# Windowed attention in a two-layer encoder trunk: the scores of its first two query blocks stand between the last projections

## The chip, the cores and the metric

The kernel runs on one core of a Trainium2 chip. The metric is the device time of one execution in microseconds (us). The profile names the engines: PE is TensorE (matmuls; PEld its weight loads), DVE is VectorE, ACT is ScalarE, POOL is GpSimd and SP issues the transfers.

## The reference

The program is a trunk of two layers on 1024 tokens of width 1024: windowed grouped-query attention, a mixture of experts, differential attention, a second mixture, and a final norm. The change touches the windowed attention alone, the first stage of the program:

```python
h = rmsnorm(x, norm_mix[0])
qkv = h @ w_qkv                       # 16 heads of queries, 4 of keys, 4 of values, 64 wide
# for each block i of 128 queries: its own 128 keys and the 128 on either side
logits = einsum('bqkgd,bskd->bkgqs', qi / 8, kb) - slopes * dist
logits = where(valid & (dist <= 128), logits, -inf)
m = max(max(logits), sink)
p = exp(logits - m)
probs = p / (sum(p) + exp(sink - m))
out[i] = einsum('bkgqs,bskd->bqkgd', probs, vb)
x = x + out @ w_o
```

## The kernel before

**The stage.** `windowed_attention` first normalises and turns the eight tiles of `x`. Then it works through four groups, one for each key/value head with the four query heads that share it. The first and the last group are written out, and the second and third are the two turns of a loop. In each group come six projections and then eight blocks of 128 queries. After the groups the output projection (`OutProjection`) adds the result to `x`.

**Six projections.** `Projections.tensor` makes projection `o` with 24 matmuls of 512 columns (eight slices of the width by three products, lines 363 to 365: every fp32 operand is kept as a high and a low part). `projections.order` gives what each makes: query heads 0 and 1, query heads 2 and 3, keys and values, first for the first 512 tokens (o = 0, 1, 2), then for the last 512 (o = 3, 4, 5). The text counts them as first to sixth. The first five eighths of the first projection stand at the group's start, and the rest (`AHEAD`) between the last blocks of the group before. ScalarE takes each result out of its PSUM bank as the high part (`q_parts` line 608, `k_hi` line 612) and VectorE takes the low part (lines 723 and 726); of the third and the sixth, ScalarE also copies keys and values together into `kvT` (line 613), a corner of the buffer `pT`. Semaphores count these steps: `proj_done`, `hi_ready`, `parts_ready`.

**PSUM.** The eight banks are `S` (four), `TB` (two) and `O` (two). Before the change the first four projections go to the banks of `S`, the fifth and sixth to `O`:

```python
projected = lambda o: S[:, o, :] if o < 4 else O[:, o - 4, :]
```

The scores of a block need all four banks of `S`, one for each query head.

**A block.** `head_scores(i)` on TensorE makes two matmuls for each head (line 790): 256 keys wide for blocks 0 and 7, 384 for the others. VectorE adds the bias and takes the maximum (`masked_scores`, line 690; its last step, `a_snk`, frees the exponentials), ScalarE takes four exponentials and that of the sink (`exponentials`, lines 596 and 598), and VectorE divides (`normalise`, line 705). `product(i)` on TensorE turns the probabilities one key tile at a time into the two banks of `TB` (line 803), ScalarE copies each turned tile into `pT` (line 630), and TensorE multiplies them with the values (line 810) into `O`; VectorE takes the block out (`heads_out`, line 712). The values are turned by `value_rows(0)` (first 512 tokens) and `value_rows(1)` (last 512): TensorE line 775 out of `kvT`, VectorE line 678.

**Order.** Each engine's order is written out by hand in its `group` function. TensorE runs the scores two blocks ahead: `head_scores(i + 2)` stands before `product(i)`. The scores of one block wait, head by head, until VectorE has read the block before (`biased`). ScalarE and VectorE also cut the next group's weights into high and low parts (`high_part`, line 405, `low_part`, line 411), a third of the slice at a time. In the last group ScalarE cuts one slice of the output weights for each block instead (line 472), with the low part on GpSimd (line 476).

## Time and profile before

| | us |
|---|---|
| median of 3 runs | 2544.45 |
| lowest, highest | 2537.21, 2546.45 |
| the profiled execution | 2540.93 |
| its span, first to last instruction | 2538.9 |
| PE busy | 2313.7 (91%) |
| DVE busy | 1866.3 (74%) |
| ACT busy | 1549.1 (61%) |
| POOL busy | 299.8 (12%) |
| mean granted TensorE clock | 0.957 of full speed |

A row of the timeline gives the start of an instruction in us from the span's start, its length, the engine, the line, what it writes and reads, how often it is repeated, and in brackets the idle time before it and what ended that. The end of a matmul is modelled and overlaps the next one's start, so the pace of TensorE is read from start to start. Buffers are named without the stage's prefix `a0_`: `a_S` are the score banks, `a_TO` are `TB` and `O` together, and the probabilities are `shared`. The four groups begin at about 31, 117, 202 and 287 us, and the output projection at 374 us.

### The profile page before, as it was taken

To read this page: it belongs to the slowest core of one execution; us is meant where nothing else is said; L and a number is where in the kernel's file an instruction comes from. 1 tells how busy PE (TensorE), PEld (TensorE's weight loads), DVE (VectorE), ACT (ScalarE), POOL (GpSimd) and SP (SyncE) were. 2 spreads that over 40 slices of the span, in tenths; PEclk is the share of its full clock that TensorE was granted. 3 is DMA by queue.
4 is the path that set the end of the run, shared out by engine and by line. 5 is a ranking of instruction groups with operands and counts; after the bars stand their busy time and mean duration, and the time that the engine had idled before them with its cause. 6 is when DMAs were issued, how large, how long until landed. Compare 5 with 4: busy or idle time off the path is not lost. (4 is left out here: it accounts for less than half of the span.)

```text
span 2538.9 us, 34343 instructions
## 1 busy us (share of the span) xinstructions
PE 2313.7 (91%) x11448; PEld 1754.4 (69%) x11448; DVE 1866.3 (74%) x2483; ACT 1549.1 (61%) x2037; POOL 299.8 (12%) x260
## 2 busy tenths in 40 slices
PE   7999989779999999948999999998967999999992
PEld 5667758657777777637888888886855777777771
DVE  5765582678898988857666676656277988989885
ACT  5554461448787777735566665555045787877872
POOL 0000020012121211130000000002001221212102
PEclk9999999979999999979999999999988999999996
DMA  3004021479999999962000000002148999999995
GB/s 125 26 22 135 25 67 53 166 248 402 393 400 397 394 401 392 401 209 93 26 25 25 25 25 17 8 25 75 45 166 288 398 401 396 402 396 396 402 388 211
DMA packets 132051, 538.62 MB, mean 212 GB/s; under 512 B 25776, under 2 KB 54576, under 8 KB 82832
## 3 DMA queue, kind: packets, MB, share of 16 engines
q1 hardware_dynamic: 113040, 470.67, 48.6%
q0 software_dynamic: 18944, 67.12, 7.6%
q8 instruction: 35, 0.57, 0.1%
q14 instruction: 32, 0.26, 0.0%
HBM read 487.54 MB, written 50.20 MB: 212 GB/s over the span
## 5 line engine op out<-in xcount | busy, mean ns | idle before, releaser
L1694 DVE TENSOR_TENSOR m_lo_gate<-m_raw_gate,m_hi_gate 128x2048 fp32r<-128x2048 f32 x132 | 297.6, 2290 | 79.9 <-ACT m_hi_gate L1689 79.0
L1694 DVE TENSOR_TENSOR m_lo_up<-shared,m_hi_up 128x2048 fp32r<-128x2048 f32 x128 | 292.4, 2286 | 3.6 <-ACT m_hi_up L1689 3.4
L1694 DVE TENSOR_TENSOR m_lo_down<-m_raw_down,m_hi_down 128x2048 fp32r<-128x2048 f32 x124 | 279.0, 2282 | 6.1 <-ACT m_hi_down L1689 6.1
L1689 ACT CAST m_hi_down<-m_raw_down 128x2048 fp32r<-128x2048 f32 x124 | 236.2, 1906 | 34.4 <-DMA m_raw_down<-in_moe_w_down_dram 30.5
L1689 ACT CAST m_hi_gate<-m_raw_gate 128x2048 fp32r<-128x2048 f32 x132 | 246.4, 1908 | 10.7 <-DMA m_raw_gate<-in_moe_w_gate_dram 10.6
L1689 ACT CAST m_hi_up<-shared 128x2048 fp32r<-128x2048 f32 x128 | 244.5, 1912 | 12.9 <-DMA shared<-in_moe_w_up_dram 12.1
L1811 PE MATMUL m_G<-m_hi_gate,m_x_hi 128*96 128x512 f32 x512 | 205.6, 402 | 11.3 <-DVE m_x_lo L1921 11.3
L1698 POOL DMA_INDIRECT m_xg<-hn_rows,m_pick x62 | 158.9, 2562 | 415.8 <-PE m_XT L1824 415.8
L1811 PE MATMUL m_U<-m_hi_up,m_x_hi 128*96 128x512 f32 x512 | 205.2, 401 | 0.0
L1812 PE MATMUL m_G<-m_hi_gate,m_x_lo 128*96 128x512 f32 x512 | 205.2, 401 | 0.0
L1813 PE MATMUL m_G<-m_lo_gate,m_x_hi 128*96 128x512 f32 x512 | 203.7, 398 | 0.0
L1812 PE MATMUL m_U<-m_hi_up,m_x_lo 128*96 128x512 f32 x512 | 201.9, 394 | 0.0
L1813 PE MATMUL m_U<-m_lo_up,m_x_hi 128*96 128x512 f32 x512 | 200.3, 391 | 0.0
L1811 PE MATMUL m_Y<-m_hi_down,m_h_hi 128*96 128x512 f32 x496 | 198.6, 400 | 0.0
L1812 PE MATMUL m_Y<-m_hi_down,m_h_lo 128*96 128x512 f32 x496 | 195.1, 393 | 0.0
L1813 PE MATMUL m_Y<-m_lo_down,m_h_hi 128*96 128x512 f32 x496 | 194.6, 392 | 0.0
L1407 DVE CUSTOM_DVE_ANT_0 shared<-a_S,a_bias 128x1024 f32<-128x1024 f32 x128 | 151.6, 1222 | 22.2 <-PE a_S L1525 11.9
L1308 ACT ACTIVATE shared<-shared 128x1024 f32<-128x1024 f32 x128 | 146.1, 1144 | 29.1 <-DVE shared L1412 27.3
L363 PE MATMUL a_S<-a1n_hi,a_w_hi 128*128 128x512 f32 x384 | 155.9, 406 | 0.0
L364 PE MATMUL a_S<-a1n_hi,a_w_lo 128*128 128x512 f32 x384 | 152.6, 397 | 0.0
L365 PE MATMUL a_S<-a1n_lo,a_w_hi 128*128 128x512 f32 x384 | 152.6, 397 | 0.0
L1892 ACT ACTIVATE m_gated<-m_G,zero_col 96x512 f32<-96x512 f32 x64 | 43.8, 684 | 157.2 <-PE m_G L1813 156.8
(385 smaller groups left out, 4989.8 us busy)
## 6 DMA issues: line engine op xcount, KB each, us to landing
m_raw_gate<-in_moe_w_gate_dram SPq DMA_DIRECT2D x128, 1024.0 KB, 9.8
shared<-in_moe_w_up_dram SPq DMA_DIRECT2D x128, 1024.0 KB, 11.9
m_raw_down<-in_moe_w_down_dram SPq DMA_DIRECT2D x124, 1024.0 KB, 10.9
out_rows<-m_y POOLq DMA_DIRECT2D x64, 384.0 KB, 8.0
a1n_rows<-in_diff_w_qkv_dram SPq DMA_DIRECT2D x21, 512.0 KB, 5.3
out_rows<-gain_b SPq DMA_DIRECT2D x1, 8064.0 KB, 37.2
x_res<-in_x_dram SPq DMA_DIRECT2D x4, 1024.0 KB, 10.0
a0n_rows<-in_swa_w_o_dram SPq DMA_DIRECT2D x8, 512.0 KB, 3.6
```

Source lines behind the costliest of these rows:

```text
L363: pe.matmul(out, left[0], right[0], start=first, stop=False)
L364: pe.matmul(out, left[1], right[0], start=False, stop=False)
L365: return pe.matmul(out, left[0], right[1], start=False, stop=last)
L1308: last = act.activation(row, row, ACT.Exp, bias=neg2[:, i % 2, c:c + 1], accum_out=sum2[:, i % 2, c:c + 1])
L1407: dve.tensor_tensor_reduce(probs[:, i % 2, c, :].rearrange("p (a b) -> p a b", a=2), S[:, 2 * c:2 * c + 2, :], bias[:, at:at + T].rearrang ...
L1689: act.copy(self.hi[w][:, cut], self.raw[w][:, cut]).then_inc(self.hi_done[w], 1)
L1694: eng.tensor_tensor(self.lo[w][:, cut], self.raw[w][:, cut], self.hi[w][:, cut].bitcast(F32), ALU.subtract)\
L1698: pool.indirect_dma_start(out=self.xg[:, :], out_offset=None, in_=self.hn_rows, in_offset=bass.IndirectOffsetOnAxis(rows, 0)).then_inc(sel ...
L1811: pe.matmul(out[n], l_hi[:, rows], r_hi[:, cols], start=(k == 0), stop=False)
L1812: pe.matmul(out[n], l_lo[:, rows], r_hi[:, cols], start=False, stop=False)
L1813: last = pe.matmul(out[n], l_hi[:, rows], r_lo[:, cols], start=False, stop=(k == K - 1))
L1892: act.activation(gated[:, :], G[0:CAP, :], ACT.Silu, bias=t.zero_col[0:CAP, :]).then_inc(gated_done, 1)
```

## The change

- Projections 4 to 6 go to other banks: the fourth to `O[0]`, the fifth to `TB[1]`, the sixth to `O[1]`. `S[3]` takes no projection any more.
- TensorE makes the scores of block 0 and the first half's value rows behind the fourth projection instead of the fifth, and the scores of block 1 behind the fifth instead of the sixth. The scores of block 2 follow the sixth at once. The second half's value rows stand behind the product of block 0, no longer before the scores of block 2.
- ScalarE takes the exponentials of block 0 behind the fourth projection's queries and those of block 1 behind the fifth's. It copies block 0's turned tiles before it takes the sixth projection out.
- VectorE does the same for its steps, and normalises block 1 before the sixth projection's low part. The low parts of the next group's weights move: the first third behind block 0's scores, the second into block 2; the last third stays in block 4.
- `kvT` lies in the other half of `pT`, and TensorE's waits for parts and value rows are set to the new order.

```diff
--- before.py
+++ after.py
@@ -524,7 +524,7 @@
         v_rows = sb("a0_v_rows", [P, NT, 2, HEAD], F32)
         probs = t.shared[:, :].rearrange("p (a b n) -> p a b n", a=3, b=QH)
         pT = sb("a0_pT", [P, 2, 3, QH * P], F32)
-        kvT = pT[:, 0, 0:2, :].rearrange("p a b -> p (a b)")
+        kvT = pT[:, 1, 0:2, :].rearrange("p a b -> p (a b)")
         bias = sb("a0_bias", [P, QH, WIN], F32)
         dist = sb("a0_dist", [P, WIN], F32)
         far = sb("a0_far", [P, WIN], F32)
@@ -546,7 +546,7 @@
 
         sink_loaded = t.sem("a0_sink_loaded")
 
-        projected = lambda o: S[:, o, :] if o < 4 else O[:, o - 4, :]
+        projected = lambda o: (S[:, 0, :], S[:, 1, :], S[:, 2, :], O[:, 0, :], TB[:, 1, :], O[:, 1, :])[o]
         proj_done, hi_ready, parts_ready = projections.done, t.sem("a0_hi_ready"), t.sem("a0_parts_ready")
         v_turned, v_rows_ready = t.sem("a0_v_turned"), t.sem("a0_v_rows_ready")
         scores, scores_seen, biased = t.sem("a0_scores"), t.sem("a0_scores_seen"), t.sem("a0_biased")
@@ -599,7 +599,15 @@
                            .then_inc(exp_done, 1)
 
 
+                    def turned_out(i):
+                        for j in range(tiles[i]):
+                            c = TILES * g + before[i] + j
+                            act.wait_ge(p_turned, c + 1)
+                            act.copy(pT[:, i % 2, j, :], TB[:, (before[i] + j) % 2, :]).then_inc(pT_ready, 1)
+
                     for o in range(6):
+                        if o == 5:
+                            turned_out(0)
                         act.wait_ge(proj_done, 6 * g + o + 1)
                         (j, n), out = projections.order[o], projected(o)
                         cols = slice(n * HALF, (n + 1) * HALF)
@@ -613,21 +621,19 @@
                             act.copy(kvT[:, cols], out).then_inc(hi_ready, 1)
                         if n == 1 and j < 2 and not last_group:
                             projections.high_part(act, g + 1, j)
-                        if o == 4:
-                            exponentials(0)
+                        if o in (3, 4):
+                            exponentials(o - 3)
 
                     for i in range(NT):
-                        if i + 1 < NT:
+                        if 2 <= i + 1 < NT:
                             exponentials(i + 1)
                         if last_group:
                             out_proj.high_weights(act, i)
                         n = 8 * g + i
                         if i >= 2:
                             act.wait_ge(pv_done, n - 1)
-                        for j in range(tiles[i]):
-                            c = TILES * g + before[i] + j
-                            act.wait_ge(p_turned, c + 1)
-                            act.copy(pT[:, i % 2, j, :], TB[:, (before[i] + j) % 2, :]).then_inc(pT_ready, 1)
+                        if i >= 1:
+                            turned_out(i)
                         if i == 3 and not last_group:
                             projections.high_part(act, g + 1, 2)
 
@@ -714,6 +720,9 @@
 
 
                     for o in range(6):
+                        if o == 5:
+                            masked_scores(2)
+                            normalise(1)
                         dve.wait_ge(hi_ready, 6 * g + o + 1)
                         (j, n), out = projections.order[o], projected(o)
                         cols = slice(n * HALF, (n + 1) * HALF)
@@ -726,23 +735,23 @@
                                 last = dve.tensor_tensor(k_lo[part, cols], out[0:64],
                                                          k_hi[0:64, cols].bitcast(F32), ALU.subtract)
                         last.then_inc(parts_ready, 1)
-                        if n == 1 and j < 2 and not last_group:
-                            projections.low_part(dve, g + 1, j)
-                        if o == 4:
+                        if o == 3:
                             masked_scores(0)
                             value_rows(0)
+                            if not last_group:
+                                projections.low_part(dve, g + 1, 0)
                             normalise(0)
-                    for i in range(NT):
+                        if o == 4:
+                            masked_scores(1)
+                    value_rows(1)
+                    heads_out(0)
+                    for i in range(2, NT):
                         if i + 1 < NT:
                             masked_scores(i + 1)
-                        if i == 0:
-                            value_rows(1)
-                        else:
-                            normalise(i)
-                        if i >= 1:
-                            heads_out(i - 1)
-                        if i == 4 and not last_group:
-                            projections.low_part(dve, g + 1, 2)
+                        normalise(i)
+                        heads_out(i - 1)
+                        if i in (2, 4) and not last_group:
+                            projections.low_part(dve, g + 1, i // 2)
                     if last_group:
                         o_part(0)
                         o_part(1)
@@ -780,7 +789,7 @@
                         n = 8 * g + i
                         a, b = blocks[i]
                         if i == 0:
-                            pe.wait_ge(parts_ready, 6 * g + 4)
+                            pe.wait_ge(parts_ready, 6 * g + 3)
                         if i == 3:
                             pe.wait_ge(parts_ready, 6 * g + 6)
                         for h in range(QH):
@@ -831,22 +840,26 @@
 
 
 
-                        if o == 4:
+                        if o == 3:
                             pe.wait_ge(parts_ready, 6 * g + 1)
                         projections.tensor(pe, out, g, o, first_group)
-                        if o == 4:
-
-
+                        if o == 3:
                             head_scores(0)
                             value_rows(0)
-                    head_scores(1)
-                    value_rows(1)
+                        if o == 4:
+                            head_scores(1)
                     for i in range(NT):
                         if i + 2 < NT:
                             head_scores(i + 2)
                         if i == 0:
+                            pe.wait_ge(v_rows_ready, 2 * g + 1)
+                            pe.wait_ge(parts_ready, 6 * g + 5)
+                        if i == 1:
+                            pe.wait_ge(parts_ready, 6 * g + 6)
                             pe.wait_ge(v_rows_ready, 2 * g + 2)
                         product(i)
+                        if i == 0:
+                            value_rows(1)
 
                 group(0, True, False)
                 with pe.Fori(1, KV - 1) as g:
```

ScalarE in the first group, from the second third of the weights on, before:

```order
L405 CAST a_w_hi<-a0n_rows 128x8x128
L593 ISA
L596 ACTIVATE shared,a_sum<-shared,a_neg 128x256 x4
L598 ACTIVATE a_exs<-a_snk,zero_col 128x4
L603 REGISTER_ALU
L612 CAST a_k_hi<-a_TO 64x512 x2
L613 COPY a_pT<-a_TO 128x512
L593 REGISTER_ALU
L596 ACTIVATE shared,a_sum<-shared,a_neg 128x384 x4
L598 ACTIVATE a_exs<-a_snk,zero_col 128x4
L629 ISA
L630 COPY a_pT<-a_TO 128x512
```

and after the change:

```order
L405 CAST a_w_hi<-a0n_rows 128x8x128
L593 REGISTER_ALU
L596 ACTIVATE shared,a_sum<-shared,a_neg 128x384 x4
L598 ACTIVATE a_exs<-a_snk,zero_col 128x4
L605 ISA
L606 COPY a_pT<-a_TO 128x512
L605 REGISTER_ALU
L606 COPY a_pT<-a_TO 128x512
L611 REGISTER_ALU
L620 CAST a_k_hi<-a_TO 64x512 x2
L621 COPY a_pT<-a_TO 128x512
```

Block 1's exponentials (384 wide) and block 0's two turned tiles stood behind the sixth projection's keys (`a_k_hi`, and `a_pT` at line 613), and now stand ahead of them.

VectorE in the first group, around the sixth projection's low part of the keys, before:

```order
L702 RECIPROCAL a_inv<-a_sum 128x4
L62 REGISTER_ALU
L705 TENSOR_SCALAR shared<-shared,a_inv 128x256 x4
L717 REGISTER_ALU
L726 TENSOR_TENSOR a_k_lo<-a_TO,a_k_hi 64x512 x2
L74 ISA
L690 ISA shared,a_top<-a_S,a_bias 128x384
```

and after the change:

```order
L708 RECIPROCAL a_inv<-a_sum 128x4
L62 REGISTER_ALU
L711 TENSOR_SCALAR shared<-shared,a_inv 128x384 x4
L726 REGISTER_ALU
L735 TENSOR_TENSOR a_k_lo<-a_TO,a_k_hi 64x512 x2
L681 REGISTER_ALU
L684 COPY a_v_rows<-a_TO 128x4x64 x2
```

Before, block 0's division (256 wide) came ahead of the keys' low part and block 1's masked scores behind it. Now block 1's division (384 wide) comes ahead of it, and the second half's value rows behind it.

TensorE in the first group, from the end of block 2's scores on, before:

```order
L790 MATMUL a_S<-a_k_hi,a_q_parts 128x384
L790 MATMUL a_S<-a_k_lo,a_q_parts 128x384
L803 MATMUL a_TO<-ident,shared 128x128 x8
L810 MATMUL a_TO<-a_pT,a_v_rows 128x512 x2
L790 MATMUL a_S<-a_k_hi,a_q_parts 128x384
```

and after the change:

```order
L799 MATMUL a_S<-a_k_lo,a_q_parts 128x384
L812 MATMUL a_TO<-ident,shared 128x128 x8
L819 MATMUL a_TO<-a_pT,a_v_rows 128x512 x2
L784 MATMUL a_TO<-ident,a_pT 128x128 x4
L799 MATMUL a_S<-a_k_hi,a_q_parts 128x384
```

Block 3's scores followed block 0's product at once, and the value turn out of `a_pT` stood ahead of block 2's scores; now it stands between block 0's product and block 3's scores.

## Rows read from the trace of the kernel before

**Rows 1.** The page: TensorE's granted clock in 40 slices, in tenths of full speed.
```profile
PEclk9999999979999999979999999999988999999996
```

**Rows 2.** Timeline of TensorE, second group, from its fifth projection to block 4.
```profile
137.49 0.40 PE L363 MATMUL a_TO<-a0n_hi,a_w_hi 128*128 128x512 f32 x1
...
143.09 0.27 PE L790 MATMUL a_S<-a_k_hi,a_q_parts 128*128 128x256 f32 x1
...
144.38 0.48 PE L363 MATMUL a_TO<-a0n_hi,a_w_hi 128*128 128x512 f32 x1
...
150.07 0.34 PE L790 MATMUL a_S<-a_k_hi,a_q_parts 128*128 128x384 f32 x1
...
151.31 0.34 PE L790 MATMUL a_S<-a_k_lo,a_q_parts 128*128 128x384 f32 x1
153.40 0.66 PE L775 MATMUL a_TO<-ident,a_pT 128*128 128x128 f32 x4 [1.75 <-ACT a_pT L613]
155.41 0.69 PE L790 MATMUL a_S<-a_k_hi,a_q_parts 128*128 128x384 f32 x1 [1.35 <-DVE a_top L690]
...
163.43 1.28 PE L790 MATMUL a_S<-a_k_hi,a_q_parts 128*128 128x384 f32 x1
...
171.65 1.04 PE L803 MATMUL a_TO<-ident,shared 128*128 128x128 f32 x8
...
174.32 1.97 PE L810 MATMUL a_TO<-a_pT,a_v_rows 128*128 128x512 f32 x4
175.72 0.74 PE L790 MATMUL a_S<-a_k_hi,a_q_parts 128*128 128x384 f32 x1
```

**Rows 3.** Timeline of TensorE, first group: fifth projection and block 3's scores.
```profile
54.03 0.40 PE L363 MATMUL a_TO<-a0n_hi,a_w_hi 128*128 128x512 f32 x1
...
78.61 0.74 PE L790 MATMUL a_S<-a_k_hi,a_q_parts 128*128 128x384 f32 x1
```

**Rows 4.** Timeline of TensorE, last group: fifth projection, block 3's scores, block 1's product.
```profile
307.79 0.40 PE L363 MATMUL a_TO<-a0n_hi,a_w_hi 128*128 128x512 f32 x1
...
332.07 0.74 PE L790 MATMUL a_S<-a_k_hi,a_q_parts 128*128 128x384 f32 x1
...
335.17 1.12 PE L810 MATMUL a_TO<-a_pT,a_v_rows 128*128 128x512 f32 x2 [0.24 <-ACT a_pT L630]
```

**Rows 5.** Busy time in four stretches; PEclk is the column behind POOL's.
```profile
69.00:79.00 10.00, 6.80 (x25) 4.74 (x25) 9.30 (x35) 5.91 (x18) 0.00 (x0) 0.83 0.00 0
150.00:166.00 16.00, 12.36 (x43) 8.96 (x43) 11.48 (x43) 9.53 (x30) 0.00 (x0) 0.68 0.00 1
...
321.00:331.00 10.00, 6.32 (x27) 4.86 (x26) 9.40 (x35) 5.90 (x16) 0.80 (x1) 0.83 0.01 2
338.00:373.00 35.00, 28.81 (x135) 18.10 (x134) 31.68 (x91) 27.63 (x70) 14.23 (x6) 1.00 0.29 91
```

**Rows 6.** Timeline of ScalarE, second group; the last row is from the last group.
```profile
151.58 1.17 ACT L612 CAST a_k_hi<-a_TO 64x512 fp32r<-64x512 f32 x2
...
157.42 0.62 ACT L596 ACTIVATE shared<-shared,a_neg 128x384 f32<-128x384 f32 x1 [4.07 <-DVE a_snk L696]
...
159.83 0.28 ACT L598 ACTIVATE a_exs<-a_snk,zero_col 128x4 f32<-128x4 f32 x1
...
172.28 1.07 ACT L630 COPY a_pT<-a_TO 128x512 f32<-128x512 f32 x2 [0.45 <-PE a_TO L803]
...
333.56 1.04 ACT L472 CAST a0n_hi<-a0n_rows 128x1024 fp32r<-128x1024 f32 x1
```

**Rows 7.** Timeline of VectorE, second group.
```profile
153.38 1.38 DVE L726 TENSOR_TENSOR a_k_lo<-a_TO,a_k_hi 64x512 fp32r<-64x512 f32 x2 [0.24 <-ACT a_pT L613]
154.79 0.56 DVE L690 CUSTOM_DVE_ANT_0 shared<-a_S,a_bias 128x384 f32<-128x384 f32 x1
...
160.50 0.15 DVE L701 TENSOR_TENSOR a_sum<-a_sum,a_exs 128x4 f32<-128x4 f32 x1
...
160.90 1.41 DVE L705 TENSOR_SCALAR shared<-shared,a_inv 128x384 f32<-128x384 f32 x4
```

## The prediction

> **What bounds the kernel now.** I begin with the granted clock on the page [rows 1]: TensorE is at full speed nearly everywhere, with dips in the third, ninth, sixteenth and later slices. The first dips lie inside the windowed attention, the only stage that the change touches. The timeline of TensorE in the second group shows where [rows 2]. Up to block 1's scores it works without a pause. Then it waits 1.75 us for ScalarE, which has to copy the last keys and values before they can be turned, and 1.35 us for VectorE, which can read block 1's scores only behind the keys' low part. The first score matmul behind that wait lasts 0.69 us where it lasted 0.34. The table by stretches says why: between 150 and 166 us the granted clock is 0.68 in the mean [rows 5]. With two levels, 2.4 and 1.2 GHz, that is 2 × 0.32 × 16 = 10.2 us at 1.2 GHz. The first and the last group have the same two waits and 2 × 0.17 × 10 = 3.4 us at 1.2 GHz [rows 5]. Everywhere else in a group TensorE is close to busy, so a group is as long as TensorE's work plus this one hole. All later stages begin behind the attention's end, so a microsecond saved here is saved at the end.
>
> The measure of the hole is the time from the start of the fifth projection's matmuls to the start of block 3's scores. Exactly the same TensorE work lies in it before and after: two projections, three sets of scores, two value turns and block 0's product, if for "after" I count from the end of the fourth projection, where block 0's scores now begin. Before, it is 163.43 − 137.49 = 25.94 us in the second group [rows 2], and the third repeats it. In the first it is 78.61 − 54.03 = 24.58 [rows 3], in the last 332.07 − 307.79 = 24.28 [rows 4].
>
> **The same stretch after the change**, worked out on the second group, with 0 at the end of the fourth projection.
> - *Scores of block 0 and the first value turn.* They cost 144.38 − 143.09 = 1.29 us behind the fifth projection [rows 2], and 1.29 behind the fourth. Their parts are the first three projections'; the third's take 1.80 + 1.38 us [rows 6, 7] of the fourth's 5.60. So the fifth projection runs from 1.29, for 143.09 − 137.49 = 5.60 us, to 6.89.
> - *Scores of block 1.* They wait for VectorE's reading of block 0, which has all of the fifth projection's 5.60 us for it; the wait is hidden. Eight matmuls: 151.31 − 150.07 = 1.24 from the first to the eighth and 0.18 for that one, 1.42. The sixth projection runs from 8.31 to 13.91.
> - *Scores of block 2*, 1.42 again, to 15.33, if VectorE has read block 1. It takes the fifth projection's low part from about 8.8, an estimate: 2.8 for the fourth's high and low part (as for the keys, without the third copy), then for block 0 the masked scores 2.1, the exponentials 2.3 and the division 1.6, each some 0.85 of the 384-wide price below. The low part is 1.4 [rows 7], then block 1 in 157.42 − 154.79 = 2.6 [rows 6, 7], so to 12.8. It is ready 1.1 us early.
> - *Product of block 0.* TensorE turns from 15.33. ScalarE has block 1's exponentials behind it by then: they start at 12.8 and take 159.83 + 0.28 − 157.42 = 2.69 [rows 6], to 15.5. The first turned tile can be copied 172.28 − 171.65 = 0.63 after the turns start [rows 2, 6], at 15.96, and both copies take 1.07 [rows 6], to 17.03. TensorE's two products take 175.72 − 174.32 = 1.40 [rows 2] and are issued by about 18.0.
> - *The new wait.* Only now does ScalarE take out the sixth projection. From its first copy of keys to VectorE's low part it takes 153.38 − 151.58 = 1.80 [rows 6, 7], so to 18.83, and the low part takes 1.38 more [rows 7], to 20.21. Block 3's scores need it and begin at about 20.28 with 0.07 for the two hand-overs. TensorE waits about 0.9 for the value turn and 1.1 for the scores; counted as the trace does it, from a product's modelled end, that is about 0.3 and 0.9. What queues behind: on TensorE block 3's scores and block 1's product; on ScalarE the sixth projection behind the turned tiles; on VectorE the second value rows and everything of block 3.
> - *VectorE in this spot.* Block 2's scores are read while they are made, from 14.3 to 16.9, and block 1 is normalised in 160.90 + 1.41 − 160.50 = 1.81 [rows 7], to 18.7. The keys' copies are there at 18.83, so this chain has 0.1 us to spare. It is the tightest spot of the new order.
>
> So the stretch is 20.28 us. **The sum:** first group 24.58 − 20.28 = 4.30. Second and third 25.94 − 20.28 = 5.66 each. Last group 24.28 − 20.28 = 4.00, less a loss behind it: ScalarE cuts a 1.04 us slice of the output weights in each block [rows 6], and the slices of blocks 0 and 1, 2.1 us, now both stand between the keys' copies and block 1's turned tiles, together with block 2's exponentials of 2.7. That puts the first copy at 17.03 + 1.8 + 4.8 = 23.6, where TensorE offers the tile at 20.28 + 1.8 (scores behind a product, the first 0.40 longer [rows 2]) + 0.6 = 22.7. Before, block 1's product waited 0.24 [rows 4]; it will wait about 0.85 more. Last group: 3.15. Together 4.30 + 2 × 5.66 + 3.15 = **18.8 us**.
>
> *Edits at no cost.* The fourth projection now goes to an `O` bank and waits for this group's first parts, which VectorE finishes during the second projection, over 5 us ahead. The weights' second third moves on VectorE into block 2 (1.2 us); GpSimd and SP's queue keep their order, and the load of the next weights waits for the last third, which stays in block 4.
>
> *Bounds.* Without any wait the stretch would be TensorE's own issue, 1.29 + 5.60 + 1.42 + 5.60 + 1.42 + 0.9 + 1.40 + 0.35 = 17.98, worth 2.3 us more in each group: 18.8 + 9.2 = 28.0 at most. From below, the clock decides. The rows show full speed kept where waits are spread: in the last 35 us of blocks TensorE was busy 28.81 us and the clock stayed at 1.00 [rows 5]. They show it lost behind 1.75 + 1.35 = 3.1 us of waiting close together [rows 2]. The new waits, about 1.2 us counted the same way, are nearer to the first, so I take full speed.
>
> A section of the Trainium skill speaks against that: "TensorE: Matmul & The Clock Gate", A second HAM failure mode: psum-queue depth-cycling, says that short idle spells between groups of matmuls, as a kernel cycles through its PSUM banks, can send the clock back and forth. By that rule the gain would be that of the first rival; the last group's blocks, with such spells and the clock at 1.00, speak against it here.
>
> **The rivals.**
> - *The clock still falls in the new hole.* Two waits within 2 us remain, ahead of dense work. The least that a fall cost in time at 1.2 GHz was 3.4 us [rows 5], which at half speed is 1.7 us where TensorE sets the pace. In all four groups: 18.8 − 6.8 = 12.0, 2544.45 − 12.0 = 2532. For it: the spell lies behind a product that itself has short waits. Against: under half of the idle time before.
> - *VectorE shows in block 2.* The tight 0.1 us goes, and the 1.2 us moved there add up in three groups: 3.7 less, 15.1, 2529. Against: VectorE was busy 11.48 of 16 us around the hole [rows 5], and TensorE has two blocks of scores as a buffer.
> - *Slower.* The clock falls in each group at block 3's scores and stays down for 10.2 us, as it did in the second and third [rows 5]. Before, much of that lay beside waits; now it would lie on dense work, 5.1 us a group, 20.4 in all, against 18.8: slower by 1.6, 2546. It decides from 4.7 us lost a group, and becomes measurable only near 8. Against: it takes a deeper hole than the old one to hold the clock down that long under dense work.
> - *Nothing arrives.* The saving is made and given back behind the attention, by a transfer or a stage with its own start: 2544. SP issues the experts' first weights only behind the attention's last step, so I see no such start.
>
> **How the numbers follow.** Against the profiled execution's 2540.93 the sum gives 2522.1; the median of the runs lies 3.5 above that execution, and gives 2525.6. I take **2524**. Chances: forecast 0.60, clock rival (in some or all groups) 0.22, VectorE 0.10, nothing 0.05, slower 0.03. The range goes from near the bound of 28 us, 2515, to the clock rival with the runs' own spread of some 5 us, 2537. A measurement can tell about 0.5%, 12.7 us, from no change. The forecast and the VectorE rival lie beyond that, the clock rival about on it: faster 0.75, same 0.22, slower 0.03.
>
> **What would show it.** In the second group of the new trace: fifth projection's first matmul about 1.3 us behind the fourth's end; no wait before block 1's and block 2's scores; a wait for `a_pT` ahead of the value turn and one for `a_k_lo` ahead of block 3's scores, under 1.2 us each; 20.3 us from the fourth projection's end to block 3's scores; a granted clock of 1.00 there; groups some 79.5 us long instead of 85; in the last group a wait near 1 us ahead of block 1's product. Wrong would be a clock below 0.9 in these stretches, a wait ahead of block 0's turns (VectorE late with the division), or block 4's scores later than 6 us behind block 3's.

## The result, and the profile after

| | before | after |
|---|---|---|
| median of 4 runs each, us | 2543.47 (2537.21 to 2546.45) | 2519.71 (2515.79 to 2521.06) |
| profiled execution, us | 2540.93 | 2520.45 |
| its span, us | 2538.9 | 2518.4 |

The ratio is 0.9906, with a 95% interval from 0.9892 to 0.992: the changed kernel is 23.8 us faster by the medians, and 20.5 by the two profiled executions.

The page's line of the granted clock, to be held against [rows 1]:

```profile
PEclk9999999799999999959999999999978999999996
```

It hardly differs, and it can't: a slice is 63 us long, a 9 stands for 90% or more, and 3.4 us at half speed leave 97%. The lower digits, the ninth and eighteenth before and the eighth and eighteenth now, and the last three in both, lie behind the attention, which ends in the sixth slice. The prediction's opening sentences, with dips in the third and sixteenth slices and the first of them inside the attention, misread it; what carried the argument are the stretches of [rows 5], to which the fence after next answers.

The timeline of TensorE in the second group of the changed kernel (start, length, engine, line, out<-in; in brackets the idle time before and who ended it). It answers to [rows 2]. The first row is the first score matmul behind the fourth projection, the zero point of the prediction's clock:

```profile
132.32 0.28 PE L799 MATMUL a_S<-a_k_hi,a_q_parts 128*128 128x256 f32 x1
...
133.63 0.47 PE L363 MATMUL a_TO<-a0n_hi,a_w_hi 128*128 128x512 f32 x1
...
139.30 0.34 PE L799 MATMUL a_S<-a_k_hi,a_q_parts 128*128 128x384 f32 x1
...
140.72 0.39 PE L363 MATMUL a_TO<-a0n_hi,a_w_hi 128*128 128x512 f32 x1
...
146.32 0.33 PE L799 MATMUL a_S<-a_k_hi,a_q_parts 128*128 128x384 f32 x1
...
147.73 1.03 PE L812 MATMUL a_TO<-ident,shared 128*128 128x128 f32 x8
149.00 1.98 PE L819 MATMUL a_TO<-a_pT,a_v_rows 128*128 128x512 f32 x4 [0.24 <-ACT a_pT L606]
151.15 0.65 PE L784 MATMUL a_TO<-ident,a_pT 128*128 128x128 f32 x4 [0.17 <-ACT a_pT L621]
152.77 0.44 PE L799 MATMUL a_S<-a_k_hi,a_q_parts 128*128 128x384 f32 x1 [0.97 <-DVE a_k_lo L735]
...
158.35 0.74 PE L799 MATMUL a_S<-a_k_hi,a_q_parts 128*128 128x384 f32 x1
```

The two waits of 1.75 and 1.35 us are gone. In their place stand 0.24, 0.17 and 0.97 us, and the first score matmul behind them lasts 0.44 us, where it lasted 0.69. The stretch that the prediction measures, from 132.32 to 152.77, takes 20.45 us; the last row says that block 4's scores follow 5.58 us later.

The granted clock by stretches answers to [rows 5] (stretch, its length, busy time of TensorE, weight loads, VectorE, ScalarE and GpSimd, granted clock, DMA share, GB/s). These four hold the hole of each group:

```profile
69.00:79.00 10.00, 8.48 (x40) 5.26 (x39) 9.56 (x37) 7.31 (x18) 0.00 (x0) 1.00 0.00 0
147.00:163.00 16.00, 14.15 (x71) 9.62 (x70) 14.95 (x50) 11.58 (x33) 0.00 (x0) 1.00 0.01 2
226.00:242.00 16.00, 14.16 (x69) 9.40 (x68) 14.94 (x51) 11.60 (x32) 0.00 (x0) 1.00 0.00 1
304.00:320.00 16.00, 13.17 (x67) 9.16 (x65) 14.92 (x49) 14.21 (x37) 4.98 (x3) 1.00 0.20 66
```

**Where the 21 us came from.** Every group has one mark, the fifth projection's start before and block 0's scores after; the time between two marks is one group. The attention ends where the output projection's first matmul starts (before, then after):

```profile
374.23 0.50 PE L363 MATMUL a_S<-a0n_hi,a_w_hi 128*128 128x512 f32 x1 [0.29 <-DVE a_w_lo L666]
```
```profile
352.80 0.50 PE L363 MATMUL a_S<-a0n_hi,a_w_hi 128*128 128x512 f32 x1 [0.29 <-DVE a_w_lo L672]
```

| | before | after | gain |
|---|---|---|---|
| first mark | 54.03 | 53.34 | 0.69 |
| first group | 83.46 | 78.98 | 4.48 |
| second group | 85.10 | 78.80 | 6.30 |
| third group | 85.20 | 78.78 | 6.42 |
| last mark to the output projection | 66.44 | 62.90 | 3.54 |
| sum | 374.23 | 352.80 | 21.43 |
| from there to the end of the span | 2164.7 | 2165.6 | -0.9 |

The gain of the first line is there ahead of everything that the change touches (in the two traces the first projection starts at 28.38 and 27.86 us), so it is taken as scatter: over all traces of this study this mark lies between 52.98 and 54.30 us. The last line is within its scatter too: over the same traces, one for each kernel, that part takes 2160.4 to 2168.3 us. A single span therefore can't show what a few us are worth, and the experiments are read at the output projection's start first, and by their medians second.

### The profile page after: what moved, and what is told of

Read it like the earlier page. It is cut to its first block and busy times, and to the rows that moved or that the text cites. A ratio compares the mean times of both kernels' runs of the same rounds, so it can differ in the third digit from the quotient of the medians.

```text
span 2518.4 us, 34348 instructions
## 1 busy us (share of the span) xinstructions
PE 2303.8 (91%) x11448; PEld 1747.6 (69%) x11448; DVE 1863.6 (74%) x2483; ACT 1551.2 (62%) x2037; POOL 309.7 (12%) x260
## 5 line engine op out<-in xcount | busy, mean ns | idle before, releaser
L1711 POOL DMA_INDIRECT m_xg<-hn_rows,m_pick x62 | 170.8, 2755 | 408.8 <-PE m_XT L1837 408.8
```

The costliest lines, as they stand in the source:

```text
L1711: pool.indirect_dma_start(out=self.xg[:, :], out_offset=None, in_=self.hn_rows, in_offset=bass.IndirectOffsetOnAxis(rows, 0)).then_inc(sel ...
```

## The experiments

Nine kernels ran. e1, e2, e6 and e7 shared one chip and its runs of the kernel before (median 2539.54), e0, e3, e4 and e5 another (2541.93), and e9 ran by itself (2541.32). Ratios are against these.

| | ratio (95%) | output projection starts | stretch in groups 1 to 4 |
|---|---|---|---|
| before | 1 | 374.23 | 24.58, 25.94, 25.95, 24.28 |
| e1, banks only | 1.0009 (0.9997 to 1.0021) | 373.15 | 24.57, 24.57, 25.94, 25.04 |
| e6, first wait filled | 0.9991 (0.9979 to 1.0003) | 372.73 | 24.58, 25.76, 24.59, 25.65 |
| e9, both waits filled | 0.9986 (0.9976 to 0.9995) | 373.01 | 24.58, 25.62, 24.58, 25.64 |
| e2, block 0 only | 0.9967 (0.9954 to 0.9979) | 365.29 | 23.26, 23.26, 23.26, 24.20 |
| e7, weights back | 0.992 (0.9897 to 0.9943) | 355.40 | 21.07, 21.17, 21.15, 20.36 |
| after, run again (e0) | 0.9913 (0.99 to 0.9927) | 353.14 | 20.34, 20.45, 20.45, 20.35 |
| e3, keys first | 0.9911 (0.9897 to 0.9925) | 355.25 | 20.33, 20.45, 20.45, 20.36 |
| e5, both first | 0.9909 (0.9894 to 0.9924) | 352.95 | 20.10, 20.10, 20.09, 20.10 |
| e4, low keys first | 0.9948 (0.9935 to 0.9962) | 361.86 | 20.22, 20.33, 20.32, 20.20 |

### What part of the change brings the gain

**e1, banks only.** The kernel before with nothing but the new banks, and the wait for the group's first parts moved to the projection that now takes `O[0]`:

```diff
-        projected = lambda o: S[:, o, :] if o < 4 else O[:, o - 4, :]
+        projected = lambda o: (S[:, 0, :], S[:, 1, :], S[:, 2, :], O[:, 0, :], TB[:, 1, :], O[:, 1, :])[o]
...
-                        if o == 4:
+                        if o == 3:
                             pe.wait_ge(parts_ready, 6 * g + 1)
```

> The kernel before with the new banks and nothing else: the fourth projection goes to O[0], the fifth to TB[1], the sixth to O[1], and TensorE's wait for this group's first parts moves from the fifth to the fourth projection; no scores, exponentials or copies are moved. My theory (the gain is the shorter chain in the hole, and the clock that stays up there; the banks only make room): the same stretch from the fifth projection's start to block 3's scores, 24.6, 25.9, 25.9 and 24.3 us in the four groups, ratio to before 1.000. Rival A (the banks themselves help or hurt, by who reads them while TensorE writes): a stretch or a projection that differs by over 0.3 us, a ratio off by over 0.002. Rival B (the clock alone brings the gain): 1.000 too, since the hole stays.

It is the kernel before, within 0.2%. The banks bring nothing of the gain; they only make room for the order. The trace has a surprise, to which I come back: in the second group the same two waits of 1.76 and 1.36 us stand in it, and yet the stretch takes 24.57 us and not 25.94, while that of the last group takes 25.04 and not 24.28. Both differ by more than the 0.3 us that the expectation named as the sign of rival A. The banks aren't needed for it: e6 and e9, with the old banks, show the like, 24.59 and 24.58 us in the third group, 25.65 and 25.64 in the last.

**e2, block 0 only.** The new banks, and block 0's scores, exponentials, reading and value turn behind the fourth projection. Block 1 stays behind the sixth:

```diff
+        projected = lambda o: (S[:, 0, :], S[:, 1, :], S[:, 2, :], O[:, 0, :], TB[:, 1, :], O[:, 1, :])[o]
...
-                        if o == 4:
+                        if o == 3:
                             exponentials(0)
...
-                        if o == 4:
+                        if o == 3:
+                            masked_scores(0)
+                            value_rows(0)
                         if n == 1 and j < 2 and not last_group:
                             projections.low_part(dve, g + 1, j)
-                            masked_scores(0)
-                            value_rows(0)
+                        if o == 3:
                             normalise(0)
...
-                        if o == 4:
+                        if o == 3:
                             head_scores(0)
                             value_rows(0)
                     head_scores(1)
+                    pe.wait_ge(parts_ready, 6 * g + 5)
                     value_rows(1)
```

> Half of the change: with the new banks, the scores, masked scores, exponentials, value rows and division of block 0 stand behind the fourth projection; block 1's scores stay behind the sixth, block 0's turned copies behind the keys. My theory: ScalarE has block 0's exponentials behind it when the sixth projection ends, so the keys come 1.4 us earlier and all behind them; the stretch from the fourth projection's end to block 3's scores is about 23.2 us (before 24.6, 25.9, 25.9, 24.3; after 20.4), the waits for a_pT and a_top are about 0.6 and 1.0 us instead of 1.75 and 1.35, and the clock stays up. Time about 2534, ratio 0.996. Rival B (the clock alone): with the clock at 1.00 the whole gain is there, 2520, ratio 0.991.

The order half of the expectation held in three groups: 23.26 us a stretch for 23.2, the first wait down to 0.44 us; the second stayed at 1.36 us, where 1.0 was expected. In the last group the stretch is 24.20 us, 0.08 less than before: there block 0's product waits for ScalarE in both kernels, 1.82 us before and 1.70 in e2. The clock half of the expectation failed. TensorE in its second group, and the first group's stretch:

```profile
149.70 0.66 PE L776 MATMUL a_TO<-ident,a_pT 128*128 128x128 f32 x4 [0.44 <-ACT a_pT L613]
151.71 0.44 PE L791 MATMUL a_S<-a_k_hi,a_q_parts 128*128 128x384 f32 x1 [1.36 <-DVE a_top L690]
...
152.19 0.51 PE L791 MATMUL a_S<-a_k_hi,a_q_parts 128*128 128x384 f32 x1
```
```profile
69.00:79.00 10.00, 8.63 (x36) 6.33 (x36) 9.22 (x37) 6.57 (x21) 0.00 (x0) 0.83 0.00 0
```

Two score matmuls run at full speed, the third lasts 0.51 us instead of 0.34: the fall comes half a microsecond behind the 1.36 us wait. 0.83 over 10 us is 3.4 us at 1.2 GHz, as in [rows 5], with under 60% of the waiting. So to halve the waiting isn't enough to keep the clock. The attention ends 8.9 us earlier than before, the whole change 21.4: moving block 1 too, with the turned copies, brings the other 12.5.

**e7, weights back.** The changed kernel with the low part of the weights' second third ahead of block 1's masked scores again, where before had it:

```diff
                         if o == 4:
+                            if not last_group:
+                                projections.low_part(dve, g + 1, 1)
                             masked_scores(1)
...
-                        if i in (2, 4) and not last_group:
-                            projections.low_part(dve, g + 1, i // 2)
+                        if i == 4 and not last_group:
+                            projections.low_part(dve, g + 1, 2)
```

> The changed kernel with one part undone: the low part of the next weights' second third stands behind the fifth projection's low part again, ahead of block 1's masked scores, instead of in block 2. My theory: 1.2 us more on VectorE ahead of block 1's scores pushes its exponentials to 149.1 instead of 147.9 in the second group, the turned copies and the keys behind them by 0.8 and block 3's scores by 0.7, in the first three groups: stretch 21.1 instead of 20.4, time 2521.8, ratio to before 0.9915. Rival (the place of that step is free, it only fills VectorE's idle time): stretch 20.4, ratio 0.9906.

Its second group (TensorE, then ScalarE):

```profile
151.05 1.98 PE L821 MATMUL a_TO<-a_pT,a_v_rows 128*128 128x512 f32 x4 [1.08 <-ACT a_pT L606]
153.20 0.66 PE L786 MATMUL a_TO<-ident,a_pT 128*128 128x128 f32 x4 [0.16 <-ACT a_pT L621]
154.71 0.44 PE L801 MATMUL a_S<-a_k_hi,a_q_parts 128*128 128x384 f32 x1 [0.85 <-DVE a_k_lo L735]
```
```profile
147.70 0.62 ACT L596 ACTIVATE shared<-shared,a_neg 128x384 f32<-128x384 f32 x1 [4.63 <-DVE a_snk L702]
...
150.42 1.07 ACT L606 COPY a_pT<-a_TO 128x512 f32<-128x512 f32 x2
```

VectorE spends 1.23 us on the weights, block 1's exponentials start that much later, and ScalarE comes to block 0's turned tiles 0.84 us late, counted from the group's mark: 21.1 us a stretch in the groups that have next weights, 20.36 in the last, which has none. The expectation held. This line of the change, which in the diff looks like tidying, is worth about 0.7 us a group, 2.3 us at the output projection with e7 against e0. Its clock stayed at 1.00, with waits of 1.08, 0.16 and 0.85 us.

### What holds the new hole

**e0**, the changed kernel once more beside e3, e4 and e5:

> The changed kernel itself, beside the three variants of it. Expected as before: ratio 0.991, stretch from the fourth projection's end to block 3's scores 20.3 to 20.5 us, clock 1.00 in the hole.

It repeated the stretches to 0.03 us, and the ratio within its interval.

**e3, keys first.** ScalarE takes the sixth projection's keys and values out before block 0's turned tiles, the old order of these two steps. The last group's first slice of output weights moves to stand with the second, so that it isn't in the hole:

```diff
                     for o in range(6):
-                        if o == 5:
-                            turned_out(0)
...
-                        if last_group:
+                        if last_group and i:
+                            if i == 1:
+                                out_proj.high_weights(act, 0)
                             out_proj.high_weights(act, i)
...
-                        if i >= 1:
-                            turned_out(i)
+                        turned_out(i)
```

> The changed kernel with one part undone: ScalarE takes out the sixth projection (keys and kvT) before it copies block 0's turned tiles, as in the kernel before. Rival (what the place of these copies decides, as the change's description has it): the copies and with them block 0's product come 1.8 us later, block 3's scores too: stretch 22.2, time up by 7. My theory after the changed kernel's trace: block 3's scores wait for VectorE, where the division of block 1 (ends 151.34 us) stands ahead of the keys' low part; TensorE has about 2 us to spare for the product. Products from 18.0 to 19.4 us behind the fourth projection's end, value turn to 19.8, scores at 20.4 as now. Stretch 20.4, same time as the changed kernel.

The stretch is the same to 0.01 us:

```profile
151.15 1.98 PE L818 MATMUL a_TO<-a_pT,a_v_rows 128*128 128x512 f32 x4 [1.49 <-ACT a_pT L606]
...
153.68 0.44 PE L798 MATMUL a_S<-a_k_hi,a_q_parts 128*128 128x384 f32 x1
```

ScalarE has the keys out at 150.60 us and VectorE, busy with block 1's division, takes them at 152.16. The wait that is printed stands ahead of the product (1.49 us), and nothing is won: VectorE's chain ends when it did. The copies' new place, a point of its own in the description of the change, is not where the gain is. The profiled execution reached the output projection 2.1 us after e0's: 0.5 us are there at the first mark, and 1.6 come in the last group (64.48 us for 62.84 from the mark on), where the clock fell at block 2's product (0.57 between 322 and 326 us). The medians differ by 1.3 us; in time the two kernels can't be told apart.

**e4, low keys first.** VectorE takes the keys' low part ahead of block 1's division:

```diff
                         if o == 5:
                             masked_scores(2)
-                            normalise(1)
...
+                    normalise(1)
                     value_rows(1)
```

> The changed kernel with VectorE's keys' low part ahead of block 1's division instead of behind it; ScalarE as in the changed kernel. My theory: the keys' copies end at 18.8 us behind the fourth projection's end, and the low part starts at 18.8 instead of 18.9, so the stretch is 20.3 and nothing else moves: same time as the changed kernel within 1 us. Rival (the division is what holds the hole open): stretch 18.9 to 19.5, 4 us less in all.

This was my worst expectation. Of the stretch itself it holds: 0.1 us shorter. But e4 is 8.65 us slower than e0 by the medians (2526.76 and 2518.11), and its attention ends 8.7 us later. The price is paid behind the stretch. TensorE, second group and last group:

```profile
156.71 1.09 PE L812 MATMUL a_TO<-ident,shared 128*128 128x128 f32 x8 [0.77 <-DVE a_v_rows L684]
...
319.93 1.94 PE L812 MATMUL a_TO<-ident,shared 128*128 128x128 f32 x8 [4.79 <-DVE a_v_rows L684]
```

Block 1's turns need the division and the value rows behind it. In the first three groups that is about 1 us each. In the last it is 4.79 us, and behind it the turns last 1.94 us instead of 1.09: the clock went too. The reason is seen on VectorE and GpSimd in the last group:

```profile
313.43 2.00 DVE L707 TENSOR_TENSOR a_sum<-a_sum,a_exs 128x4 f32<-128x4 f32 x1
...
315.68 3.49 DVE L711 TENSOR_SCALAR shared<-shared,a_inv 128x384 f32<-128x384 f32 x4
```
```profile
313.02 2.39 POOL L476 TENSOR_TENSOR a0n_lo<-a0n_rows,a0n_hi 128x1024 fp32r<-128x1024 f32 x1 [279.13 <-ACT a0n_hi L472]
316.54 2.41 POOL L476 TENSOR_TENSOR a0n_lo<-a0n_rows,a0n_hi 128x1024 fp32r<-128x1024 f32 x1 [1.13 <-ACT a0n_hi L472]
```

An addition of 128x4 numbers takes 2.00 us where it takes 0.16 elsewhere, and ends with GpSimd's subtraction, at 315.4. The division's four instructions take 3.49 us where they take 1.41 [rows 7], and they end 0.2 us behind GpSimd's second subtraction. Together that is 1.8 and 2.1 us more. In the changed kernel the last group's division of block 1 runs from 307.51 to 308.92 us, and GpSimd begins at 309.71. Its later blocks pay too, as those of the kernel before do: in both, five small additions of the last group take 0.8 to 2.1 us. What is new in e4 is that block 1's division, which its turns wait for, is held too.

So block 1's division ahead of the keys is a needed part of the change, in the last group above all: from its mark to the output projection e4 takes 68.61 us for e0's 62.84, in each of the first three groups 0.9 to 1.0 us more than e0.

**e5, both first**: both orders turned, e3's edit and e4's together.

> Both orders turned round at once: ScalarE takes out the sixth projection before block 0's turned tiles, VectorE makes the keys' low part before block 1's division. In the last group the first slice of the output weights is cut behind block 2's exponentials. My theory: the two chains only give way together. Low part ready at 18.8 us behind the fourth projection's end, block 0's product from 18.0 to 19.4, value turn to 19.8, block 3's scores at 19.8 instead of 20.4: 0.6 less in the first three groups, nothing in the last, where block 1's product waits longer for the slices; 2 us in all, about 2518 where the changed kernel has 2520. Rival (block 0's copies must stand first): 22.2 as in the other run, 7 us more.

The stretch falls to 20.10 us, not to 19.8:

```profile
150.43 1.98 PE L818 MATMUL a_TO<-a_pT,a_v_rows 128*128 128x512 f32 x4 [1.49 <-ACT a_pT L606]
152.25 0.60 PE L783 MATMUL a_TO<-ident,a_pT 128*128 128x128 f32 x4
152.60 0.42 PE L798 MATMUL a_S<-a_k_hi,a_q_parts 128*128 128x384 f32 x1
```

No wait is printed ahead of the scores: behind ScalarE's copies, TensorE's own issue now ends last. I had taken 1.40 us for the product, from [rows 2], where scores follow it. From 150.43 to 152.25 it is 1.82 with the value turn behind it: the 0.4 us that the first score matmul otherwise carries (0.74 us long instead of 0.34) are paid by whatever follows. So e3 (keys taken out earlier) wins 0.0 us in the stretch, e4 (their low part made earlier) 0.1 and e5 (both) 0.3: ScalarE's keys and VectorE's division end within 0.2 us of each other, and a third path is only some 0.3 us shorter. It is the longest in e5: ScalarE's exponentials, keys and turned tiles, for which the product still waits 1.49 us, and then TensorE's own issue. No run relieves ScalarE of that work, so what the hole would be without this path isn't shown; the prediction's bound of 17.98 us is 2.1 us away.

The expectation had 2 us less in all. The first three groups, from mark to mark, give 0.25 to 0.38 us each, and the last takes 0.8 back (63.61 us for 62.84), with waits of 0.53 and 1.42 us ahead of block 2's turns and product. In time e5 can't be told from the changed kernel; no run here is measurably faster than that.

### What the clock did

**e6, first wait filled.** The kernel before with seven matmuls into `TB[1]`, which nobody reads, behind block 1's scores. They fill the 1.75 us wait and add nothing to the path:

```diff
                     head_scores(1)
+                    for _ in range(7):
+                        pe.matmul(TB[:, 1, :], k_hi[:, 0:P], q_parts[:, 0, 0:HALF], start=True, stop=True)
                     value_rows(1)
```

> The kernel before, with seven more matmuls of 512 columns on TensorE behind block 1's scores in each group, written to the free bank TB[1] and never read: about 1.5 us of the 1.75 us wait is filled with work, no other engine's order is changed. My theory: the granted clock stays at 1.00 in the hole, but the chain over ScalarE and VectorE is as long as before. In the first and last group nothing is gained, since block 0's product waits for ScalarE's copies either way; in the second and third the product's two multiplications and block 3's first scores run at full speed, 1.9 us a group. Time about 2539.7, ratio 0.9985. Rival B (the clock alone): most of the 24 us, ratio 0.991. Rival C (the clock does not matter at all): 1.000.

**e9, both waits filled.** The same, and five more of them into `TB[0]` behind the value turn, once its bank is read:

```diff
                     value_rows(1)
+                    pe.wait_ge(v_rows_ready, 2 * g + 1)
+                    for _ in range(5):
+                        pe.matmul(TB[:, 0, :], k_hi[:, 0:P], q_parts[:, 0, 0:HALF], start=True, stop=True)
```

> The kernel before with both waits of the hole filled: seven more matmuls of 512 columns behind block 1's scores (into TB[1]) and five behind the second value turn (into TB[0], once its value rows are read), none of them read. The first fill alone left the clock to fall in two of the four groups, and where it stayed up the stretch was 24.6 us as in the first group of the kernel before. My theory (the clock's share is what the second and third group of the kernel before have over 24.6, and the time at 1.2 GHz in block 3): clock 1.00 in the hole of every group, stretch 24.6 in the first three, the output projection starts at about 370.5 us instead of 374.2, ratio 0.9985. So 17 of the 21 us that the change saves up to there are the shorter chain. Rival (the clock is worth more than that): output projection's start at 366 or less.

The ratios came out as expected (0.9991 and 0.9986 for 0.9985, though e6's interval includes 1), the mechanism only in part: e9 was to reach the output projection at 370.5 us and reached it at 373.01. The stretches of e9 in the second and the third group:

```profile
150.00:166.00 16.00, 13.59 (x60) 9.30 (x58) 12.14 (x45) 9.37 (x30) 0.00 (x0) 0.89 0.00 0
236.00:252.00 16.00, 13.33 (x63) 8.62 (x61) 14.53 (x56) 9.88 (x28) 0.00 (x0) 1.00 0.00 0
```

The clock stayed up in the first and the third group and fell in the second and the last, in e6 just so. Up to block 0's product the second and the third group of e9 read alike, with waits of 0.15, 0.18 (0.20 in the third), 0.67 and 1.41 us. Then the product, in the one and in the other:

```profile
160.32 3.44 PE L810 MATMUL a_TO<-a_pT,a_v_rows 128*128 128x512 f32 x4 [1.41 <-ACT a_pT L630]
162.78 1.31 PE L790 MATMUL a_S<-a_k_hi,a_q_parts 128*128 128x384 f32 x1
...
245.21 1.98 PE L810 MATMUL a_TO<-a_pT,a_v_rows 128*128 128x512 f32 x4 [1.41 <-ACT a_pT L630]
246.63 0.74 PE L790 MATMUL a_S<-a_k_hi,a_q_parts 128*128 128x384 f32 x1
```

This fall lies on the product, where nothing hides it. It costs 162.78 − 160.32 − (246.63 − 245.21) = 1.04 us up to block 3's scores, and 0.6 more from the first of them on, where it lasts 1.31 us for 0.74. e1's second group lost the clock for as long, but earlier:

```profile
150.00:166.00 16.00, 11.30 (x52) 8.44 (x51) 13.31 (x51) 10.47 (x32) 0.00 (x0) 0.89 0.00 1
```
```profile
158.00 1.16 PE L803 MATMUL a_TO<-ident,shared 128*128 128x128 f32 x8
160.50 1.98 PE L810 MATMUL a_TO<-a_pT,a_v_rows 128*128 128x512 f32 x4 [1.34 <-ACT a_pT L630]
```

Its fall lies on block 2's scores. The turns and the product are at full speed again, TensorE still waits 1.34 us for ScalarE, and the stretch is 24.57 us, that of full speed. So here a fall of 3.5 us costs nothing ahead of a wait and 1.6 to 1.7 us on a product: from mark to mark, e9's second group takes 84.89 us and its third 83.22, e1's third 84.80 and its second 83.19. Before's middle groups, at 1.2 GHz for 10.2 us [rows 5], had both.

The groups whose clock stayed up give the price from mark to mark. e9's third takes 305.27 − 222.05 = 83.22 us; before's middle groups take 85.10 and 85.20. The slow clock cost them 1.9 and 2.0 us, and the first group nothing (83.46 there, and 83.46 with the clock up in e9). Of the 21.4 us of the change that makes 3.9 for the clock, 0.7 for the scatter at the start, and 16.8 for the waits: about 4.4 in each of three groups and 3.5 in the last. For the last no kernel of the old order kept its clock, so that its 3.5 us hold nothing for the clock is argued from where the fall lay: ahead of the product, which ran at full speed behind 1.82 us of waiting. The split rests on one execution of each kernel. What the other executions of e6 and e9 did no trace shows, so their ratios are no clean price of the clock.

## Why the prediction held, point by point

**The order on TensorE** is right to 0.1 us. With 0 at 132.32: the fifth projection at 1.31 (predicted 1.29), block 1's scores at 6.98 (6.89), the sixth projection from 8.40 to 14.00 (8.31 to 13.91), the turns at 15.41 (15.33). No wait stands ahead of block 1's and block 2's scores.

**The hole**: 20.34, 20.45, 20.42 and 20.36 us against 20.28. ScalarE and VectorE in it, answering to [rows 6, 7]:

```profile
145.24 0.62 ACT L596 ACTIVATE shared<-shared,a_neg 128x384 f32<-128x384 f32 x1 [3.37 <-DVE a_snk L702]
...
148.36 1.07 ACT L606 COPY a_pT<-a_TO 128x512 f32<-128x512 f32 x2 [0.42 <-PE a_TO L812]
149.32 1.18 ACT L620 CAST a_k_hi<-a_TO 64x512 fp32r<-64x512 f32 x2
150.51 0.59 ACT L621 COPY a_pT<-a_TO 128x512 f32<-128x512 f32 x1
```
```profile
147.01 0.56 DVE L696 CUSTOM_DVE_ANT_0 shared<-a_S,a_bias 128x384 f32<-128x384 f32 x1 [1.81 <-PE a_S L799]
...
149.93 1.41 DVE L711 TENSOR_SCALAR shared<-shared,a_inv 128x384 f32<-128x384 f32 x4
151.25 1.37 DVE L735 TENSOR_TENSOR a_k_lo<-a_TO,a_k_hi 64x512 fp32r<-64x512 f32 x2
```

Exponentials start at 12.92 (12.8), the first turned copy at 16.04 (15.96), the low part of the keys at 18.93 (18.83), and the waits ahead of the value turn and of block 3's scores are 0.17 and 0.97 us for 0.3 and 0.9. One thing inside is wrong, and it did no harm: the keys should have ended last, with VectorE 0.1 us ahead of them. The copies are done at 151.10, and the division, by its last record, at 151.34, 19.02 for the predicted 18.7: VectorE is last. The step is "block 2's scores are read while they are made, from 14.3"; VectorE began at 14.69, 0.69 us behind the first score matmul. The prediction named this as the tightest spot, and a tie within 0.2 us is what e3, e4 and e5 found.

**The clock** stayed at 1.00 in all four stretches, and the first rival (2532) did not come. The reason given for it, that smaller waits keep the clock, holds for this kernel but is no rule that I could have relied on: e2 lost the clock behind 0.44 and 1.36 us, e9 in its second group behind waits of at most 1.41 us, and e7 kept it with 1.08 and 0.85. The trace of the kernel before could have said so. The prediction gives its last group the same two waits as the others, and that is a misreading; its first wait is 0.51 us, and 1.82 us stand ahead of its product:

```profile
322.46 0.66 PE L775 MATMUL a_TO<-ident,a_pT 128*128 128x128 f32 x4 [0.51 <-ACT a_pT L613]
...
330.65 1.98 PE L810 MATMUL a_TO<-a_pT,a_v_rows 128*128 128x512 f32 x4 [1.82 <-ACT a_pT L630]
```

So 3.4 us at 1.2 GHz followed there on 0.51 and 1.35 us of waiting, not on 3.1 us. That full speed held wasn't the luck of one execution either: in the traces of the changed kernel, e0, e3, e5 and e7 it is 1.00 in all twenty stretches. Why it holds there and not in e2 is not shown. The section of the Trainium skill that the prediction weighed ("TensorE: Matmul & The Clock Gate", A second HAM failure mode: psum-queue depth-cycling) says that short idle spells between groups of matmuls can send the clock back and forth. The traces of e2, e6 and e9 agree with it, that of the changed kernel doesn't: 0.24, 0.17 and 0.97 us, and 1.00 in each group. A chance of 0.22 for that rival was not too much.

**The sum** is short by 1.9 us inside the attention's groups, 20.7 for 18.8, and the step at fault is a term, the right mechanism with a size too small: "second and third 25.94 − 20.28 = 5.66 each" measured 6.30 and 6.42. The stretch stops at the start of block 3's scores, and the slow clock's price does not. In [rows 2] the first of these matmuls lasts 1.28 us, in the first group 0.74 [rows 3]: it stands behind a product still running at half speed. Block 4's scores before:

```profile
169.86 0.74 PE L790 MATMUL a_S<-a_k_hi,a_q_parts 128*128 128x384 f32 x1
```

From block 3's to block 4's scores it was 169.86 − 163.43 = 6.43 us before and is 5.58 now, 0.85 less. Of these, 6.43 − 5.86 = 0.57 us are the slow clock's, with 175.72 − 169.86 = 5.86 for the next block at full speed, and could have been read from the same timeline. The other 0.28 are won in the first group too (5.87 and 5.60 us): block 3's first score matmul no longer stands behind a product and lasts 0.44 us for 0.74. A mark at which a slow stretch is still going on cuts off part of its price. The last group brought 3.54 for 3.15: its wait ahead of block 1's product is

```profile
313.70 1.12 PE L819 MATMUL a_TO<-a_pT,a_v_rows 128*128 128x512 f32 x2 [0.90 <-ACT a_pT L606]
```

0.90 us for the predicted 1, and 0.66 more than before [rows 4]. Behind the stretch only 42.54 − 42.16 = 0.38 us were lost, not 0.85; which later wait took in the rest wasn't followed.

**From the sum to the time.** The profiled execution came out at 2520.45 for 2522.1. The forecast of 2524 leaned towards the median of before, which lay 3.5 us above its profiled execution; after's median lies 0.7 below its own. That is 1.6 us by the sum and 2.6 by this choice, and the second part is scatter, since the part behind the attention alone varies by 8 us over the traces.

**The other rivals.** VectorE does show, as the last to end in the hole, but by 0.1 to 0.2 us a group and not 3.7 us in all. e7 shows that the 1.2 us which the change moved would have cost 0.7 us a group in their old place. Behind the attention the change gave back no more than that part's scatter (0.9 us of 8). The slower case had no start: no clock fell.

## What to carry to other kernels

When two engines' chains meet in one wait, relieve each alone and both together before speaking of the bottleneck, and look for the path that is longest then: here 0.0, 0.1 and 0.3 us, and a third path behind the two. When a step is put later on a chain that doesn't bound the stretch, follow who needs it next, and which engine will be at work beside it by then: e4 won 0.1 us in the hole and lost 8.7 behind it. And take the price of a slow clock from whole periods, from one mark to the same mark a round later, not from a stretch that ends while it still runs.

## What the hardware showed that was not expected

- The same instructions and the same waits let the clock fall in one group and not in the next: e6 and e9 in the second and last, not in the first and third. The last groups of e3 and e5 are a second such pair: behind waits of 0.54 and 1.41 us the clock fell in e3 (0.57 between 322 and 326 us), and behind 0.53 and 1.42 it stayed at 1.00 in e5. The fall lasted 3.4 to 3.5 us in most places, 6.7 in e1's last group and 10.2 in before's second and third. What decides stays open; it isn't the hole's own waits alone, since those of e9's second and third group read alike.
- GpSimd's subtraction held VectorE up: 2.00 us for an addition of 0.16 us. GpSimd's own instruction took 2.35 to 2.46 us in every row of e4, so that it was held in turn isn't seen. The changed kernel has such a case in five blocks of the same group, for instance

```profile
319.98 0.55 DVE L696 CUSTOM_DVE_ANT_0 shared<-a_S,a_bias 128x384 f32<-128x384 f32 x1
...
320.57 1.56 DVE L700 TENSOR_TENSOR a_top<-a_top,a_sink 128x4 f32<-128x4 f32 x1
```
```profile
319.76 2.35 POOL L476 TENSOR_TENSOR a0n_lo<-a0n_rows,a0n_hi 128x1024 fp32r<-128x1024 f32 x1 [4.17 <-ACT a0n_hi L472]
```

where the masked scores, with one input in PSUM, keep their 0.55 us beside the same subtraction of GpSimd, and the small addition behind them waits for its end. The Trainium skill ("SBUF — State Buffer", Who interferes with whom) says that a VectorE instruction with two inputs in SBUF contends with a GpSimd instruction that reads SBUF, and that one with at most one such input doesn't, unless it runs in one of VectorE's two-port modes, where whoever issues first keeps the other out for its whole instruction. The additions (two inputs in SBUF) and the masked scores (one) agree. e4's division has one tile of SBUF as its input and was held all the same; whether it ran in such a mode no row shows.
- A product of fp32 tiles costs its follower: 1.40 us to the next start and 0.40 more in the first score matmul behind it, or 1.82 us to the next start when turns follow.
